# Page means between the duos of the first half's attention, and the sample's ranks on four heads a half: a one-layer decoder step on one core

## The reference, cut to what matters

```python
def _block(x, ...):
    h = _rmsnorm(x, norm_mix_w)
    z, xbc, dt_raw, q, kv_c, kv_s, kv_w, nsa_g, br_g = _split_proj(h @ w_in)
    y_ssm, conv_new, ssm_new = _mamba_branch(z, xbc, dt_raw, ...)
    o_attn, win_new = nsa_core(q, kv_c, kv_s, kv_w, gates)
    y_attn = o_attn.reshape(b, T, ATTN_WIDTH) @ w_attn_branch
    ...
    x = x + merged @ w_out
    x = x + _peer_tokens(_rmsnorm(x, norm_ffn_w), peer_wq, peer_sub_keys, peer_u, peer_v)

def _nsa_sample(pool_cmp, pool_sel, win_buf, page_table, q, ...):
    past_cmp = pool_cmp[page_table].reshape(b, past // CMP_BLOCK, CMP_BLOCK, KV_HEADS, 2, ATTN_HEAD_DIM).mean(axis=2)
    ...
def _peer(h, peer_wq, peer_sub_keys, peer_u, peer_v):
    q = (h @ peer_wq).reshape(n, PEER_HEADS, 2, PEER_HALF)
    s = jnp.einsum('nhcd,hckd->nhck', q, peer_sub_keys)
    top_s, top_i = lax.top_k(s, PEER_TOPK)
    cand_s = (top_s[:, :, 0, :, None] + top_s[:, :, 1, None, :]).reshape(n, PEER_HEADS, -1)
    best_s, best_pos = lax.top_k(cand_s, PEER_TOPK)
    g = jax.nn.softmax(best_s, axis=-1)
    act = jax.nn.gelu(jnp.einsum('nd,nhkd->nhk', h, peer_u[experts]))
    return jnp.einsum('nhk,nhkd->nd', g * act, peer_v[experts])
```

## Time and profile before

| | |
|---|---|
| median of the three runs | 3095.3 us |
| the profiled execution's own time | 3088.66 us |
| its span, first to last instruction | 3086.9 us |
| PE, DVE, ACT, POOL busy | 2161.9, 1541.5, 609.6, 1485.5 us |
| moved by DMA | 842.83 MB, mean 273 GB/s |
| group a ends, group b ends | about 692, about 1833 us |
| stage_pages | 2161.9 to 2250.6 us |
| stage_sample_query begins, first gather of `rest` | 2716.4, 2842.25 us |

### The profile page before, as it was taken

One profiled execution on the slowest core, in us unless ns is written; L12 is line 12 of the kernel. 1 busy time (PEld: TensorE's weight loads), 2 busy tenths in 40 slices (PEclk: granted clock), 3 DMA queues, 4 the chain that ended last, 5 costly groups with the idle time before them and its releaser, 6 DMA issues. The chain is left out here.

```text
span 3086.9 us, 31860 instructions
## 1 busy us (share of the span) xinstructions
PE 2161.9 (70%) x11034; PEld 1373.3 (44%) x11034; DVE 1541.5 (50%) x3886; ACT 609.6 (20%) x1714; POOL 1485.5 (48%) x1509
## 2 busy tenths in 40 slices
PE   8999978878867798956789966634356766663044
PEld 6788855566655475522345543322124443120010
DVE  4421033176978972455420358997455564018810
ACT  3331044022332200123430123311011111000000
POOL 0210000044245675667654567657546665554775
PEclk9899969887978898878999976656578888777566
DMA  6223411407636899989999949869989998996998
GB/s 228 82 82 119 145 50 54 161 19 264 225 124 238 308 409 349 361 343 358 349 345 378 370 168 386 291 208 344 418 313 362 362 373 287 393 377 248 358 374 298
DMA packets 209127, 842.83 MB, mean 273 GB/s; under 512 B 25608, under 2 KB 32072, under 8 KB 189448
## 3 DMA queue, kind: packets, MB, share of 16 engines
q0 software_dynamic: 170912, 644.95, 56.2%
q1 hardware_dynamic: 38056, 195.83, 17.1%
HBM read 821.54 MB, written 23.28 MB: 274 GB/s over the span
## 5 line engine op out<-in xcount | busy, mean ns | idle before, releaser
L3216 POOL DMA_INDIRECT e_ring<-in_peer_u,e_idx x576 | 682.4, 1185 | 492.4 <-DVE e_dot L3365 252.3
L3365 DVE CUSTOM_DVE_ANT_0 e_ring<-e_ring,e_h 128x1024 f32<-128x1024 f32 x576 | 702.4, 1249 | 181.0 <-DMA e_ring<-in_peer_u,e_idx 136.1
L3216 POOL DMA_INDIRECT e_ring<-in_peer_v,e_idxT x576 | 585.8, 1017 | 371.0 <-issue 156.2
L3283 PE MATMUL ps<-e_ring,e_wz 128*32 128x512 f32 x2304 | 354.3, 736 | 317.0 <-DMA e_ring<-in_peer_v,e_idxT 292.2
L3283 PEld LDWEIGHTS ps<-e_ring,e_wz 128*32 128x32 f32 x2304 | 75.8, 125 | 527.3 <-issue 523.0
L1621 POOL CAST ra_atf<-ra_at 128x32 f32<-128x32 uint32 x8 | 1.7, 212 | 254.4 <-DVE ra_hit L1614 254.4
L358 PE MATMUL ps<-hTb,wb 128*128 128x320 f32 x384 | 114.3, 455 | 0.0
L1876 PE MATMUL ps<-ss_bsel,ss_xde 64*128 64x512 f32 x64 | 53.7, 932 | 64.7 <-DVE room L1926 26.6
L358 PEld LDWEIGHTS ps<-hTb,wb 128*128 128x128 f32 x384 | 75.5, 201 | 30.3 <-issue 5.1
L1456 DVE TENSOR_REDUCE apb_nmax<-ps 128x2 f32<-128x768 f32 (+1 forms) x32 | 34.8, 1089 | 98.1 <-PE ps L1380 42.6
L3408 DVE TENSOR_TENSOR e_x<-e_x,ps 128x512 f32<-128x512 f32 x10 | 6.4, 683 | 150.1 <-PE ps L3283 107.5
(11 more groups left out here) (728 smaller groups left out, 4368.3 us busy)
## 6 DMA issues: line engine op xcount, KB each, us to landing
wb<-in_weights SPq DMA_DIRECT2D x51, 1024.0 KB, 4.9
e_ring<-in_weights SPq DMA_DIRECT2D x48, 1024.0 KB, 4.9
wb<-in_late_weights SPq DMA_DIRECT2D x6, 2048.0 KB
room<-in_late_weights SPq DMA_DIRECT2D x6, 2048.0 KB, 16.7
h<-in_weights SPq DMA_DIRECT2D x11, 1024.0 KB
xs<-in_weights SPq DMA_DIRECT2D x10, 1024.0 KB
e_ring<-in_peer_u,e_idx POOLq DMA_INDIRECT x576
e_ring<-in_peer_v,e_idxT POOLq DMA_INDIRECT x576
```

Of the source, the lines that this page charges most:

```text
L3216: nc.gpsimd.indirect_dma_start(out=self.ring[:, place % self.NR, :], out_offset=None, in_=k.peer_u if kind == "u" else k.peer_v, in_offset ...
L3283: last = nc.tensor.matmul(k.ps[32 * b:32 * b + 32, self.SUMS + i, :], self.wz[:, at:at + 32], self.ring[:, self.v_at[n] % self.NR, 512 * i ...
L3365: v.tensor_tensor_reduce(uu, uu, self.h[:, tile % 2, :], 1.0, 0.0, ALU.mult, ALU.add, self.dot[:, tile % 2, t:t + 1]).then_inc(self.dotted, 1)
```

## The change

1. The page stage is no longer in the sample's part. Its work is a class `Pages`, called from the hooks of group a's attn_prompt: four duos for one sequence. Behind `score`, `turn` and `value` of duo 4b PE does 8 of the 16 matmuls, behind those of duo 4b+1 the other 8, behind those of 4b+3 the fold. ACT copies the sums ahead of the exps of duo 4b+2, and the means ahead of those of the next duo 4b. POOL gathers the first two sequences' pages in cmp_prompt and the others at duo 4b+2. SP stores each sequence's means in DRAM. Pages come into `e_ring`'s slots 6 to 13, sums into PSUM banks 6 and 7, means into bank 4.
2. The weights of group a have three places in the ring instead of seven, five in all.
3. In sbs SP loads the means from DRAM into `zs` behind the last weights, and the block waits for it.
4. The 30 tokens of the page stage go to sbs (28 to 32), attn (180 to 190), sba (26 to 30), sample_out (28 to 32) and sample_query (60 to 68).
5. In `stage_sample_query` partitions 0 to 63 hold heads 0 to 3 and partitions 64 to 127 heads 4 to 7. The `peer_wq` pieces are cut so that each half of the weights carries two heads of either half. DVE ranks four times instead of eight; hooks are 9 instead of 13; one copy of the queries instead of two, one of the scores instead of two per half. `stage_routes` copies `named` in two parts, and a memset of `named` is new on DVE.

```diff
@@ stage_cmp_prompt, GpSimd
             nc.gpsimd.memset(both[:], 0.0).then_inc(zeroed, 1)
+            if g.first:
+                for b in range(2):
+                    gather_pages(nc, k, k.cache_cmp_kv, b, k.page_room[b], k.page_ahead[b])
@@ stage_attn_prompt, TensorE (the same on GpSimd, ScalarE and VectorE)
                 if i < N:
                     ex.pe(i)
+                    if g.first:
+                        pages.pe(i)
@@ stage_sample_branch, SyncE
+            if not which:
+                sp.dma_start(k.zs[0:NCMP_S].rearrange("p (b c) -> p b c", b=NB),
+                             k.means_dram.rearrange("b n c d -> n b (c d)")).then_inc(means_in, 16)
+                sp.wait_ge(means_in, 16)
@@ in place of stage_pages
+class Pages:
+    STEPS = 4
...
+        if step == 2 and b + 2 < NB:
+            pool.wait_ge(self.averaged, b + 1)
+            gather_pages(nc, k, k.cache_cmp_kv, b + 2, k.page_room[b % 2], k.page_ahead[b % 2])
...
+    def pe(self, i):
+        nc, k, pe, N = self.nc, self.k, self.nc.tensor, NCMP_S
+        b, step = divmod(i, self.STEPS)
+        if i == 0:
+            pe.wait_ge(self.ind_done, 1)
+        if step < 2:
+            if step == 0:
+                pe.wait_ge(k.page_ahead[b % 2], 16 * (b // 2 + 1))
                 if b >= 2:
+                    pe.wait_ge(self.parted, b - 1)
+            for r in range(8 * step, 8 * step + 8):
+                c = N * (r % 4)
+                last = nc.tensor.matmul(self.sums(b)[c:c + N], self.ind[:], k.page_room[b % 2][:, KVW * r:KVW * r + KVW],
+                                        start=(r < 4), stop=(r >= RUN - 4), skip_group_check=True)
+            if step == 1:
+                last.then_inc(self.averaged, 1)
+        if step == 3:
+            pe.wait_ge(self.parted, b + 1)
...
+            nc.tensor.matmul(self.means(b), self.fold[:], self.part[:, b % 2, :], start=True,
+                             stop=True).then_inc(self.summed, 1)
+
+    def act(self, i):
+        act, a = self.nc.scalar, self.nc.scalar
+        b, step = divmod(i, self.STEPS)
+        if step == 2:
+            act.wait_ge(self.averaged, b + 1)
+            if b >= 2:
+                act.wait_ge(self.summed, b - 1)
+            a.copy(self.part[:, b % 2, :], self.sums(b)).then_inc(self.parted, 1)
+        if step == 0 and b:
+            self.copy(b - 1)
...
+    def store(self, sp):
+        for b in range(NB):
+            sp.wait_ge(self.copied, b + 1)
+            sp.dma_start(self.k.means_dram[b], self.mean[:, b % 2]).then_inc(self.stored[b % 2], 16)
@@ stage_sample_query
-        HOOKS = 5 + PH
+        HOOKS = 5 + NH
...
-                for c in range(2):
-                    if half:
-                        pe.wait_ge(s_copied, c + 1)
-                    for m in range(4):
-                        last = mm(k.ps[:, 2 + c, P * m:P * m + P], qT[:, half, c, m].rearrange("p a n -> p (a n)"),
-                                  skT[:, 8 * half + 4 * c + m, :], start=True, stop=True)
-                    last.then_inc(scored, 1)
+                for m in range(4):
+                    for c in range(2):
+                        head = NH * c + 2 * half + m // 2
+                        last = mm(k.ps[NS * c:NS * c + NS, 2 + half, P * m:P * m + P], qT[:, half, m, NS * c:NS * c + NS],
+                                  skT[:, 2 * head + m % 2, :], start=True, stop=True)
+                last.then_inc(scored, 1)
...
-            for h in range(PH):
+            for h in range(NH):
...
+            dve.wait_ge(ex.routed_v, S - 1)
+            own(v.memset(ex.named[:, S % 2, :], 0.0))
@@ Weights
-                     for g, n in (("a", 2 + k.ex.NR // 2), ("b", 4))}
+                     for g, n in (("a", 5), ("b", 4))}
...
-        self.places += [ring[:, 2 * D * i:2 * D * i + 2 * D] for i in range(k.ex.NR // 2)] if g.first else [k.h[:], k.xs[:]]
+        self.places += [ring[:, 2 * D * i:2 * D * i + 2 * D] for i in range(3)] if g.first else [k.h[:], k.xs[:]]
@@ build
-                stage_pages(nc, k)
@@ allocate
+    k.page_room = [k.ex.ring[:, 6 + 4 * i:10 + 4 * i, :].rearrange("p r n -> p (r n)") for i in range(2)]
...
-                   state=80, mix=30, sbs=28, pages=30, cmp=22, attn=180, sba=26, sample_out=28, sample_query=60)
+                   state=80, mix=30, sbs=32, cmp=22, attn=190, sba=30, sample_out=32, sample_query=68)
```

More of the change, by code:

```diff
@@ L1347, in stage_attn_prompt, with _ @@
         k.w.enter(0)
+        if g.first:
+            pages = Pages(nc, k, ctx)
+            assert N == NB * pages.STEPS
         block = ctx.enter_context(nc.Block(no_gpsimd_drain=True))
+        @block.sync
+        def _(sp):
+            if g.first:
+                pages.store(sp)
         def weights(u):
@@ L1363, in _ @@
                 ex.pool(i)
+                if g.first:
+                    pages.pool(i)
         @block.tensor
@@ L1430, in _ @@
                     ex.act(i)
+                    if g.first:
+                        pages.act(i)
                     n = width(i)
@@ L1447, in _ @@
                                              scale=wgt[:, u:u + 1]).then_inc(scaled, 1)
+            if g.first:
+                pages.copy(NB - 1)
         @block.vector
@@ L1484, in _ @@
                     ex.dve(i)
+                    if g.first:
+                        pages.dve(i)
                     give(i)
@@ L2268, in _ @@
-        @block.vector
-        def _(dve):
-            own = Link(dve, own_s)
-            own(nc.vector.tensor_tensor(fold[:], k.ident[:, 0:N], k.ident[:, N:2 * N], ALU.add))
-            own(nc.vector.tensor_tensor(fold[:], fold[:], k.ident[:, 2 * N:3 * N], ALU.add))
-            nc.vector.tensor_tensor(fold[:], fold[:], k.ident[:, 3 * N:4 * N], ALU.add).then_inc(folded, 1)
-            for i in range(2 * NB):
-                ex.dve(i)
-        ex.close()
+        self.stored = [sem(f"stored{i}") for i in range(2)]
@@ new lines, in dve, with sums, means @@
+    def dve(self, i):
+        if i == 0:
+            v, k, fold, N = self.nc.vector, self.k, self.fold[:], NCMP_S
+            own = Link(v, self.own_s)
+            own(v.tensor_tensor(fold, k.ident[:, 0:N], k.ident[:, N:2 * N], ALU.add))
+            own(v.tensor_tensor(fold, fold, k.ident[:, 2 * N:3 * N], ALU.add))
+            v.tensor_tensor(fold, fold, k.ident[:, 3 * N:4 * N], ALU.add).then_inc(self.folded, 1)
+    def sums(self, b):
+        return self.k.ps[:, 6 + b % 2, 0:KVW]
+    def means(self, b):
+        return self.k.ps[0:NCMP_S, 4, KVW * (b % 2):KVW * (b % 2) + KVW]
@@ new lines, in act, with copy @@
+    def act(self, i):
+        act, a = self.nc.scalar, self.nc.scalar
+        b, step = divmod(i, self.STEPS)
+        if step == 2:
+            act.wait_ge(self.averaged, b + 1)
+            if b >= 2:
+                act.wait_ge(self.summed, b - 1)
+            a.copy(self.part[:, b % 2, :], self.sums(b)).then_inc(self.parted, 1)
+        if step == 0 and b:
+            self.copy(b - 1)
+    def copy(self, b):
+        act, a = self.nc.scalar, self.nc.scalar
+        act.wait_ge(self.summed, b + 1)
+        if b >= 2:
+            act.wait_ge(self.stored[b % 2], 16 * (b // 2))
+        for i, half in enumerate((keys_of, values_of)):
+            last = a.copy(self.mean[:, b % 2, i, :].rearrange("p (g d) -> p g d", g=KVH), half(self.means(b)))
+        last.then_inc(self.copied, 1)
@@ L3327, in stage_routes @@
         best, expert = (t[:].rearrange("p h k -> p (h k)") for t in (k.best, k.expert))
-        a.copy(self.named[:, tile % 2, :], expert)
         n = self.ups(tile)
-        for lo in range(0, P, n if tile == S else P):
+        for lo in range(0, P, n):
             r = slice(lo, lo + rows(tile))
-            a.copy(self.idx[r, tile % 2, 0:n], expert[r, lo:lo + n])
-            last = a.copy(self.rw[r, tile % 2, 0:n], best[r, lo:lo + n])
-        last.then_inc(self.staged, 1)
+            a.copy(self.named[r, tile % 2, lo:lo + n], expert[r, 0:n])
+        a.copy(self.idx[:, tile % 2, 0:n], expert[:, 0:n])
+        a.copy(self.rw[:, tile % 2, 0:n], best[:, 0:n]).then_inc(self.staged, 1)
     def square(self, tile):
@@ L3503, in late_pieces @@
     pieces += [block(w_out[:, 512 * i:512 * i + 512]) for i in range(2)]
-    pieces += [block(peer_wq[512 * i:512 * i + 512, D * half:D * half + D]) for half in range(2) for i in range(2)]
+    of_heads = [np.concatenate([peer_wq[:, D * c + 512 * half:D * c + 512 * half + 512] for c in range(2)], axis=1)
+                for half in range(2)]
+    pieces += [block(w[512 * i:512 * i + 512]) for w in of_heads for i in range(2)]
     return np.stack(pieces)
```

159 lines of the change are left out of this document (55 added, 104 removed).

## The result

The changed kernel takes 3054.5 us (median of 4 runs, 3039.9 to 3056.3); the kernel before, beside it, 3094.9 us (3092.7 to 3104.9). The ratio is 0.9848, 95% interval 0.9819 to 0.9876: 1.5% faster, about 40 us less. The forecast was 3046 us, a gain of 49.7. Every ratio here is of runs in the faster of two states; that leaves out one run, of e7_sums_third_duo, which took 5828 us. The profiled executions have spans of 3086.9 and 3054.6 us, so the two traces differ by 32.3 us.

What follows compares the result with a forecast made beforehand. TensorE was taken to bound the first half, DMA gathers the rest. Second half -88 + 38 + 2 - 18.7 = -66.7, first half +17: 3095.3 - 49.7 = 3046 us, 8-in-10 range 3024 to 3070.

Steps and rivals of the forecast that it cites:

- The page stage goes: Second half: removing the page stage, with its 8 page gathers and 31 expert gathers, saves its 88 us.
- the next term, cmp: Cmp, second half: its 22 tokens add up to 12 dots on VectorE, mostly in idle time; 2 us from 0 to 14.
- 30 tokens at 38 us: Second half: the page stage's tokens cost 25.6 us for 20 outside the sample's attention, 12.4 for 10 inside; together 38.
- The hole: End of the query: with four-head ranks ending ahead of the tokens, the first gather follows the last sum; -18.7 us.
- The first half: First half: page matmuls, folds and small waits, mainly in the attention, cost 17 us, from 8 to 31.
- half the pages at each level: First half's attention: four pages at the lower clock cost 3.7 us each, four at the upper 1.4; 20.4 us, taken as 15.
- The first rival: TensorE stays at the upper clock level, or the sample's attention absorbs its ten tokens; 3034 to 3037 us, chance 0.17.
- Five places: First half: weights with five ring places instead of nine still land in time; cost nothing.
- Group b: Group b, whose time the forecast left unchanged: 0 us.
- the second: The query still ends by its ranks, or cmp and the sample's attention by chains of their own; 3062 us, chance 0.15.
- The third: Bytes move but stages keep their time per token by chains; only the query's hole closes; 3094 us, chance 0.05.
- the fourth: Five weight places starve TensorE in the first half, making the kernel slower; 3111 us or more, chance 0.03.

Runs made afterwards that it cites:

- e7_sums_third_duo: The changed kernel with a page's second 8 matmuls behind duo 4b+2 instead of 4b+1; ratio 0.9778 to the kernel before, 2956.9 us.
- e5: The changed kernel run again unaltered, beside other experiments; ratio 0.9817 to the kernel before, 2967.1 us.
- e12: The changed kernel run once more unaltered, beside the last experiments; ratio 0.9845 to the kernel before, 3043.6 us.
- e8: The kernel before with the changed kernel's token shares, its page stage kept in place but without tokens; ratio 0.9994 to the kernel before.
- the first set: The first of three sets of experiments, run beside the kernel before, which took 3020.1 us there (median of 16 runs).
- the third: The last of three sets of experiments, run beside the kernel before, which took 3092.8 us there (median of 15 runs).
- e10: The kernel before with 8 matmuls, their sums unread, added behind every second duo of the first half's attention, 128 in all; ratio 0.9990.
- e1: The kernel before with only the sample's ranks changed, four heads on either half of the partitions; ratio 0.9949, 3003.8 us against 3020.1.
- e4: The changed kernel with only 4 of each page's 16 matmuls, all behind duo 4b; ratio 0.9783 to the kernel before.
- e3: The kernel before with only the first half's weight places changed, five instead of nine; ratio 1.0015 to the kernel before.
- e6: The changed kernel with 56 tokens in the query instead of 68, the other 12 past the limit; ratio 0.9752 to the kernel before, 2946.7 us.

## Why the prediction was right, and where its terms were off

The time lies in the range of 3024 to 3070, and in the forecast's own of 3032 to 3060. Beside kernels of their own set the changed one gains 50.0 and 49.2 us in the medians (e5, e12), so the 49.7 is close. The main mechanism was as told: the page stage's time goes, its bytes move into idle time, the tokens cost their share of a full queue, and the hole closes. Part of the closeness is luck: the first half cost 10.3 us less than forecast and cmp 5.9 more, two misses that partly cancel. Group b's 14.9 and the 4.5 of the sample's attention, which make the pair of traces differ by less, are of the size of the scatter there. Its steps:

- **The page stage goes: -88.** Its length was read rightly, what it was worth was not. The error is in the next term, cmp, put at 2 us out of 0 to 14 because only its dots were counted; it grew by 7.9. The 3.7 MB that the page stage drained for sbs moved there, and cmp takes 51.0 to 51.3 us in every kernel without the stage, 42.1 to 43.2 in every kernel with it. The stage's own rows said so: 36.7 MB against the 33.0 that its list of gathers gives.
- **30 tokens at 38 us.** The 12 in sbs, sba and out cost 16.1 for 15.4. In it lies the load of the means, put at nothing: sbs takes 45.3 us with it and 43.5 in e8 without. The load landed 17.4 us after its issue and 17.7 us before the stage ended, so nothing waited for it. But it was issued with the last weights of the stage and shared the queue with them: these landed 14.3 us after their issue, in e8 12.2, and TensorE's last chunk, which needs them, began 1.6 us later. So what the load cost was not its landing but the delay of those weights. The ten in the sample's attention cost 16.9 in the two traces; in the first set it is 315.2 and 312.6 against 303.6 and 304.9, 8 to 12 us, and in the third 350 to 356 against 345.4 (e10), 5 to 10. So 12.4 was a little high for most traces, and the 4.5 us above it in the pair are within the scatter of that stage.
- **The hole: -18.7.** Right as a mechanism and in size: 17.8 us alone (e1), the ranks 13.4 us under the last sum where 14 were forecast, the gather 1.15 us behind the sum where 1.05 was. Query and rest gained 7.2 for the 8.5 forecast. The cover of 14 us came out right though its terms did not: counted from the stage's start, the first scores come 20 us later than before and not 10, and both the routes and the last sum come 5 to 6 us later than forecast.
- **The first half: +17.** The half grew by 6.7 us, below the range of 8 to 31, and the attention by 7.5, to 96.9 us where 102 to 108 were looked for. The same code scatters here: over the traces the attention takes 89.4 to 93.9 us without pages and 95.1 to 97.5 with them, and in the pair ssd took 4.9 us less at a clock of 0.97 instead of 0.86, unchanged though it is. The step that failed is "half the pages at each level", from the level of 0.50 in the earlier trace rows: with the pages' matmuls the level in that half of the stage is 0.89. The first rival had this case at 8 us and was given 0.17, since no row tied the level to the work. Traces tie it: 0.57 or 0.58 in all four kernels without added matmuls, 0.74 with a quarter of them (e4), 0.89 to 0.93 with all behind 4b and 4b+1, 0.96 with the second 8 behind 4b+2 (e7), 1.00 with 8 behind every second duo (e10). The Trainium skill, TensorE: Matmul & The Clock Gate, section What's actually happening, calls the throttled state the default that activity releases; these levels agree with it. The price of a page at the upper level, 1.4, was right: a duo of step 4b+1 takes 3.29 or 3.72 us for 2.76 and the fold's 3.27, together 1.0 or 1.5 us.
- **Five places: 0.** Right (e3: +0.15%, interval -0.08 to +0.39; no wait on weights). The 6 to 8 us that e3's first half is longer in its one trace lie mostly in the attention, with its clock.
- **Group b: 0.** The pair of traces has +14.9 there, 13.4 of it in the attention. In the first two sets that stage takes 243 to 247 us in kernels of the old kind and 242 to 246 in those of the new; the third has 270 in the old (e10) and 268, 275 and 279 in the new. So the change is not shown to cost anything there, and the scatter of this stage alone is as large as the miss. A cost of a few us in it can't be excluded by these runs.

One reading of the page was off too: in the first quarter of the span the DMA engines are not "a third to half busy" but run from 0 to 7 tenths; no term rests on it.

The rivals: of the second, the ranks are out, since they end 13.4 us ahead of the tokens, and cmp's growth has another cause (e8). The third, that the bytes move and the time does not, falls with the result and with e5 and e12; the fourth, that weights run dry, with e3.

## What to carry to other kernels

Before a stage is taken out, add up the bytes that its own instructions ask for and compare them with what it moved: the difference belongs to a neighbour and comes back there. Where a limit ends a stream, let the last tokens ahead of it stand behind the work that opens it: 12 tokens moved past the limit were worth 18 to 20 us of stages, 13.5 to 15.6 of it ahead of the first gather past the limit; the rest has no cause shown. And where TensorE runs at its lower level in a loop of short matmuls, work put into its idle time can be free or better in that loop, though in e10 the whole time shows nothing of it; put it behind the step that leaves TensorE idle (e7), not behind the one that fills it.

## What was not expected of the hardware

- 128 added matmuls of fp32 made the loop around them shorter, 83.9 us for 89.4, by a granted clock of 1.00 instead of 0.58.
- GpSimd's gather instruction takes 0.94 us while VectorE runs no dot. One that starts during a dot ends 0.81 us after the dot's end (the median over the last 64 u in each of eight traces), and so takes up to 1.9 us. How the two engines stand to each other moves the mean from 975 ns (e6) to 1131 (e5).
- The same kernel takes 3017 to 3020 us in two sets and 3093 to 3095 in the other comparisons, on the same chip in the first and the third. Of the 61 us between the traces of e3 and of the kernel before, 57 lie in the two stages where attention and gathers run together (the sample's attention 305 against 343 us) and 12.5 in query and rest; the first half goes the other way by 6.5. Why, no run shows.
